# A hybrid retention and HGRN2 layer on eight cores: loads split over two DMA queues, and four more x tiles transposed by DMA

## What is computed

```
h = rmsnorm(x) * g_pre
u = h @ w_in                                   # 1024 -> 4096 columns
rq, rk, rv, rg, hq, hf, hi, hg = split(u, 8)   # 512 columns each, 4 heads of 128
# retention: rotary(rq), rotary(rk), per-head decay, causal, with a 128 x 128 state per head
# HGRN2:     f = lb + (1 - lb) * sigmoid(hf); k = 1 - f; gated causal recurrence, 128 x 128 state per head
o = concat(silu(rg) * headnorm(o_ret), silu(hg) * headnorm(o_hgrn))
y = x + rmsnorm(o @ w_out) * g_post
```

## Time and profile before

| | us |
|---|---|
| median of 3 runs | 373.36 (373.01 to 375.12) |
| the profiled execution, its own time | 374.44 |
| its span, slowest core (cores 365.5 to 372.9) | 372.9 |
| PE busy | 348.3 (93%) |
| ACT busy | 267.5 (72%) |
| DVE busy | 250.6 (67%) |
| POOL busy | 166.2 (45%) |
| mean DMA rate | 134 GB/s, 49.79 MB |

### The profile page before, as it was taken

The page is one execution under the profiler, slowest core; times in us unless marked ns, Lnnn a source line. Parts: engine busy times, 40 slices in busy tenths (PEclk is TensorE's granted clock), DMA queues, the critical chain, the costliest instruction groups (busy, mean ns, idle before and its releaser), DMA issues.

```text
span 372.9 us, 8138 instructions; the slowest of 8 cores (365.5 to 372.9 us)
## 1 busy us (share of the span) xinstructions
PE 348.3 (93%) x2307; PEld 183.1 (49%) x2307; DVE 250.6 (67%) x402; ACT 267.5 (72%) x810; POOL 166.2 (45%) x249
## 2 busy tenths in 40 slices
PE   7896989999999999999999998989879999999972
PEld 5752444454545555545455554435434445555531
DVE  2546377356888848889786776756764888877534
ACT  3655154789789998978868989667678768677661
POOL 5858822314744246463334531423434744443442
PEclk9599899999999999999999999999999999999988
DMA  7899999999313043446218256787893131634372
GB/s 188 176 158 164 197 178 187 257 215 173 100 37 107 22 148 62 84 128 144 98 31 142 57 106 153 226 224 199 149 203 104 28 71 32 141 87 115 132 206 114
DMA packets 48014, 49.79 MB, mean 134 GB/s; under 512 B 32193, under 2 KB 37441, under 8 KB 47970
## 3 DMA queue, kind: packets, MB, share of 16 engines
q1 hardware_dynamic: 43328, 36.64, 38.9%
q0 software_dynamic: 4496, 12.58, 20.2%
q10 hardware_dynamic: 146, 0.04, 0.1%
HBM read 42.05 MB, written 10.09 MB: 140 GB/s over the span
## 4 chain that ended last, share of the span: by engine, by line
PE 70%; DMA 18%; issue 3%; POOL 2%; DVE 2%; SPq 2%; ACT 1%; ACTq 0%; DVEq 0%; POOLq 0%
PE bank L782 27%; PE bank L882 20%; PE bank L1152 12%; DMA Wc<-w_c 10%; DMA ogT<-og 2%; DMA xr<-xp 2%; DMA xT<-xbf 2%; PE bank L1007 2%; PE bank L960 2%; PE bank L996 2%; PE bank L998 1%; DMA xs<-xp 1%; PE bank L755 1%; SPq L1187 1%; PE bank L1393 1%
## 5 line engine op out<-in xcount | busy, mean ns | idle before, releaser
L882 PE MATMUL bank<-Wc,xT 128*128 128x512 bf16 x512 | 120.7, 382 | 3.4 <-DVE QT L801 3.0
L782 PE MATMUL bank<-xT,Wq 128*128 128x512 bf16 (+3 forms) x656 | 121.2, 338 | 1.9 <-DMA xT<-xbf 1.9
L782 PEld LDWEIGHTS bank<-xT,Wq 128*128 128x128 bf16 x656 | 55.2, 98 | 60.5 <-issue 3.6
L882 PEld LDWEIGHTS bank<-Wc,xT 128*128 128x128 bf16 x512 | 48.6, 98 | 56.7 <-issue 5.9
L1152 PE MATMUL bank<-Wo,ogT 128*128 128x512 bf16 x224 | 54.5, 387 | 6.0 <-DMA ogT<-og 3.6
L928 ACT ACTIVATE og<-otg,rsq 128x128 bf16<-128x128 f32 (+1 forms) x120 | 38.1, 390 | 5.7 <-POOL rsq L911 4.6
L835 POOL TENSOR_TENSOR KT<-tF 128x512 bf16<-128x512 f32 (+1 forms) x20 | 17.6, 879 | 46.6 <-DVE tF L827 42.6
L796 DVE TENSOR_TENSOR bank<-bank,rotb 128x512 f32<-128x512 f32 (+1 forms) x40 | 24.0, 604 | 21.1 <-ACT tB L794 7.5
L903 ACT ACTIVATE junk<-bank 128x128 bf16<-128x128 f32 (+1 forms) x136 | 35.4, 274 | 1.8 <-PE bank L1079 1.1
L1152 PEld LDWEIGHTS bank<-Wo,ogT 128*128 128x128 bf16 x224 | 21.2, 99 | 30.3 <-issue 8.8
L911 POOL TENSOR_TENSOR rsq<-msq,mhalf 128x8 f32<-128x8 f32 (+2 forms) x21 | 30.6, 1456 | 3.2 <-ACT og L1156 0.4
(11 more groups left out here) (141 smaller groups left out, 555.8 us busy)
## 6 DMA issues: line engine op xcount, KB each, us to landing
xr<-xp SPq DMA_DIRECT2D x18, 512.0 KB, 4.9
yp<-xr SPq DMA_DIRECT2D x16, 512.0 KB, 3.1
xs<-xp SPq DMA_DIRECT2D x10, 512.0 KB, 7.3
Wc<-w_c POOLq DMA_DIRECT2D x8, 512.0 KB, 21.5
Wq<-w_q POOLq DMA_DIRECT2D x7, 512.0 KB, 20.8
rotb<-rot_p SPq DMA_DIRECT2D x4, 512.0 KB, 6.1
Wo<-w_o POOLq DMA_DIRECT2D x4, 512.0 KB, 46.7
xs<-xp POOLq DMA_DIRECT2D x2, 512.0 KB, 28.6
```

Source lines behind the costliest of these rows:

```text
L782: ins = e.matmul(banks[bk][:, c0:c1], lhsT=Wq[:, pc, kc, :], rhs=xT[:, kc, c0:c1], start=(kc == 0), stop=(kc == 7))
L882: ins = e.matmul(banks[bk][0:L, :], lhsT=xT[:, kc, j * L:(j + 1) * L], rhs=Wc[:, seg, kc, :], start=(kc == 0), stop=(kc == 7))
```

## The change

The planner's model of DMAs gets two hardware queues, SP and ACT, each with a pipe for loads; a DMA transpose on SP gets a serial price of 1200 ns of its own; a GpSimd transfer that is still running slows loads by 4 and transposes by 2. The x loads from the ninth on, and all residual loads, are issued from ScalarE in place of SyncE. `XDMA` becomes 8. The semaphore of the rotary table is split by block.

```
                     if name == "dma_start_transpose":
                         self.cost += 1250.0
-                        self.lat += 1900.0
-                        self.nbytes += 345000
+                        self.lat += 1850.0
+                        self.nbytes += 378000
...
-        pipe = {POOL: 0.0, SP: 0.0}
+        pipe = {POOL: 0.0, SP: 0.0, ACT: 0.0}
+        landed = {SP: 0.0, ACT: 0.0}
...
                 rate = 245.0 if fin < 12000.0 else 315.0
+                crossbar = o["cost"] > 1000.0 and e == SP
+                slow = 1.0
+                if e != POOL and pipe[POOL] > fin + 2500.0:
+                    slow = 2.0 if crossbar else 4.0
+                    pipe[POOL] += o["nbytes"] / rate
                 if e == POOL:
                     beg = max(fin + 1000.0, pipe[POOL], min(pipe[SP], fin + 4000.0))
                     pipe[POOL] = beg + o["nbytes"] / rate
                     dlat = pipe[POOL] - fin + 1600.0
-                elif pipe[POOL] > fin + 2500.0:
-                    beg = max(fin + 1000.0, pipe[SP])
-                    pipe[SP] = beg + 4.0 * o["nbytes"] / rate
-                    pipe[POOL] += o["nbytes"] / rate
-                    dlat = pipe[SP] - fin + 1200.0
+                elif crossbar:
+                    pipe[e] = landed[e] = max(fin + 650.0, landed[e]) + 1200.0 * slow
+                    dlat = pipe[e] - fin
                 else:
-                    beg = max(fin + (200.0 if o["cost"] > 1000.0 else 1000.0), pipe[SP])
-                    pipe[SP] = beg + o["nbytes"] / rate
-                    dlat = pipe[SP] - fin + (600.0 if o["cost"] > 1000.0 else 1200.0)
+                    pipe[e] = max(fin + 1000.0, pipe[e]) + slow * o["nbytes"] / rate
+                    landed[e] = pipe[e] + 1100.0
+                    dlat = landed[e] - fin
...
-        XDMA = 13
+        XDMA = 8
...
-            xid = S.op(POOL if 4 < state["nx"] <= 8 else SP, lambda e: e.dma_start(out=xbuf[0:L, :], in_=xrows), writes=[xkey],
+            xid = S.op(POOL if 4 < state["nx"] <= 8 else SP if state["nx"] <= 4 else ACT, lambda e: e.dma_start(out=xbuf[0:L, :], in_=xrows), writes=[xkey],
                        dma_key=xkey + (state["nx"] > 8,) if state["nx"] > 4 else xkey)
...
-            S.op(SP, lambda e: e.dma_start(out=xr[slot][0:L, :], in_=xrows), writes=[("xr", slot)], dma_key=("xr", slot),
+            S.op(ACT, lambda e: e.dma_start(out=xr[slot][0:L, :], in_=xrows), writes=[("xr", slot)], dma_key=("xr", slot, "e"),
                  deps=[state["sc0"]])
...
-                    rid = S.op(SP, lambda e: e.dma_start(out=rotb[0][:, :, 0:d["nt"]], in_=rot_p[b]), writes=[("rot", 0)], dma_key=("rot", 0))
+                    rid = S.op(SP if b < 2 else SP, lambda e: e.dma_start(out=rotb[0][:, :, 0:d["nt"]], in_=rot_p[b]), writes=[("rot", 0)],
+                               dma_key=("rot", 0, b < 2))
```

## The result

The change makes the kernel slower: median 385.11 us of four runs (383.73 to 404.0) against 373.19 us of four runs before (372.18 to 375.12), a ratio of 1.030 [1.024, 1.037]. Now and then the cores of a die show a lower granted clock and the execution is longer, as in that of 404.0 us; every ratio leaves such executions out, but the medians given in microseconds include them. The profiled execution took 385.91 us, its span 384.0 us on core 3; the median of the eight cores' spans went from 367.95 to 380.95 us, so this is a loss on every core and not on one. The lines of the printed functions have moved down by four (L725 is L729, L746 is L750, L764 is L768, L782 is L786, L882 is L886, L1113 is L1117).

The account below looks back on a forecast made before the run. PE, busy 93% of the span, was taken as the bound, with waits for DMA transposes. From the median 373.36 us, minus 1.80, minus 1.38 and plus 0.80 gave 371.0 us; 8-in-10 range 366.5 to 377.5.

Parts of the forecast that it names:

- Four tiles leave PE: Block 2's x tiles 9 to 12 stop being transposed on PE: four times 0.45 us off the chain, minus 1.80 us.
- Four DMA transposes come: Block 2's x tiles are transposed by DMA, landing 3.4 to 6.7 us after issue: cost 0 to 0.6 us, taken as 0.
- 26 loads go from SP to ACT: Block 3's last x load, issued at 261.74 us, can start up to 1.38 us earlier from ACT's queue: minus 1.38 us.
- The three ogT waits I leave as they are: PE's three waits for transposed branch output between 220 and 280 us, 3.6 us, were taken as unchanged.
- What the loads cost on ACT: Issuing 26 loads is hidden except two residual loads in the last stretch, at 0.425 us each: plus 0.80 us.
- Rival A: The split brings no earlier data, as loads and transposes share engines or another wait replaces it: 372.4 us, chance 0.28.
- Rival B: ACT is held by residual loads waiting for store landings, PE finds no free bank: 3.8 us wait, 376.2 us, chance 0.30.
- Rival C: PE's DMA waits from 220 to 280 us all go, 5.5 us back: 366.1 us, chance 0.08.
- No term below comes from the clock: Granted clock was 1.00 in every regime listed but the last, so the clock was given no term.
- My sign for being wrong altogether: PE's idle time would grow in a stretch in which PE was full before the change.

## Why the prediction was wrong

*Four tiles leave PE, minus 1.80*: right in kind. The PE transposes at the x line shrink from forty, 2.84 us, to one tile's eight, 0.40 us, and ACT's copies to one; windows of lines 759 and 768 alone, PE with PEld and then ACT, with clock, DMA share and GB/s:

```profile
93.00:132.00 39.00, 0.40 (x8) 0.28 (x8) 0.91 0.59 109
```

```profile
93.00:132.00 39.00, 0.59 (x1) 0.91 0.59 109
```

The one copy that stays is the decode tile's; the text had said none. With the loads on SP the 1.80 us came to nothing in the time (1.000 and 1.003): it was given back in those orders. In the first, with the old prices, PE stands 1.6 and 0.8 us for DVE in the stretch, on all eight cores, in the second 1.4 to 1.8 us for ACT.

*Four DMA transposes come, 0 to 0.6*: wrong. I took the last tile of block 2 and the landings of block 3. The first two tiles go out at 87.74 and 94.20, at or beside the stretch whose share of 1.03 stood in the earlier trace rows, and landed after 16.71 and 11.8 us:

```profile
L750 SPq DMA_TRANSPOSE xT<-xbf x8: 1217/1330/4016, 87.7 to 286.4; - x8
...
DMA to landing us min/median/max: 3.1/5.1/16.7
```

I had also asked only who needs xT, not who needs xbf back. With the loads on SP no wait of PE for xT stands in the stretch on any core, in either kernel, though landings of up to 12.9 us do. It is the split that turns the late landing into a stall.

*26 loads go from SP to ACT, minus 1.38*: this is the step that failed, by its sign. "On SP this takes away a place in line" is true both ways. I had read the line as something that the loads suffer from the earlier trace rows; it also kept the loads from starting beside the transposes that PE waits for. In the order of before, moving the loads costs 1.9%, some 7 us, where I had minus 1.38. "The three ogT waits I leave as they are" fell with it: from 3.6 us to 9.2 and 10.0 on the slowest cores.

*What the loads cost on ACT, plus 0.80*: the price of an issue is smaller than taken, 0.334 us by the median against 0.425, and no run isolates the tail:

```profile
L1117 ACTq DMA_DIRECT2D xr<-xp x16: 329/334/376, 146.3 to 375.0; - x16
```

*Rival A* came nearest in its mechanism, that the split brings no earlier data, but it forecast 372.4 us, no change. The Trainium skill, "DMA: Bandwidth & Descriptors", section "Issuing engines are not separate DMA queues", says that DMAs started by different engines run on the same 16 engines and interleave, and that only the time of issuing is saved. The runs agree, in that no split kernel is faster, and go further: where a load starts right beside a transpose that it used to follow, the landing goes from 4 to 7 or 10 us, so the split can lose. I had named the sharing and then priced it at the 1.38 us given back.

*Rival B* had the sign and the first half of the path: ACT stands, and PE finds no bank. Its wait was another. In the changed kernel ACT doesn't wait for a store of `yp` on the slowest core, and over the eight cores once, 2.0 us; it waits 12.2 us for transposes, at the buffer (7.1 to 14.6 over the cores). B's price was 3.8 us; the kernels differ by 11.9. And from 220 to 280 us the longest of PE's waits, 4.5 us, is for the transpose itself and not for ACT. *Rival C*'s 5.5 us of DMA waits do go in a kernel with new prices and no split (0.42 us of idle time left), and the time is still that of before within its interval. The 5.5 us were those of the slowest core; the median core had 2.10 to give.

The *clock* was in no term. "No term below comes from the clock" held of the trace of before; after, 3.51 + 3.00 us of the 16 in the two stretches went to the 1.2 GHz level; on the slowest core it stands right after PE's two longest waits. My sign for being wrong altogether didn't show: PE stays full from 132 to 220 and from 280 to 350 us. The loss came where it already waited.

## What to carry to other kernels

A single DMA queue is also an order, and it protects what was issued first: before loads move to a second queue, list the latency-critical transfers of the first one and ask which loads will now go out right beside them, and whether those can be held back by a microsecond or two (no run here tries that). Price a transfer by landings from the stretch where it will be issued, for the first of the moved tiles and not only for the one whose slack is easy to read, and ask who waits to write its source as well as who reads its result. When a change redraws an order, run its parts in the old order too: with the order kept, moving the loads alone told the queue from the planner.

## What the runs showed of the hardware

The queues of the run with one residual load on ACT, 262 to 280 us (packets, MB, share):

```profile
q1 hardware_dynamic: 4573, 2.28, 73.8%
...
q10 hardware_dynamic: 144, 0.52, 11.3%
```

One queue's packets are of 0.5 KB on average (2.28 MB / 4573), the other's of 3.6 KB. The Trainium skill, "DMA: Bandwidth & Descriptors", section "Queues, rings and completion order", says that an engine goes round its queues a packet at a time; by that a queue of small packets would lose out to one of large packets, which would fit the longer landings. It stays a guess: no run here shows the turns themselves, or that the profile counts the packets that the Trainium skill means, and the load put ahead on the same queue explains most of the delay without them.

Under the weight stream, on the eight cores, the slowest xT transpose issued between 80 and 100 us took 8.2 to 12.9 us to land with the loads on SP (three kernels) and 10.9 to 20.7 us with the loads on ACT (three kernels). And a pause of PE can cost more than its length: after the waits of 5.7 and 4.5 us, eight matmuls took 3.41 and 3.57 us in place of 1.73. Not every pause does: with the split alone, PE of core 0 waits 3.6 us at one place between 220 and 280 us, and the granted clock of the stretch is 1.00.
